# Layer 0's attention woven into its in-projection, modulation weights in half-sized parts, one copy moved

## The reference

```python
mod = silu(c) @ ada_w[i] + ada_b[i]              # 1024 -> 6 x 1024: sh1, sc1, g1, sh2, sc2, g2
h = rms_norm(x, norm1_g[i]) * (1 + sc1) + sh1
q, k, v = split(h @ w_in)                        # 1024 x 3072
a = softmax(q1 k1' - slopes*dist) - lam * softmax(q2 k2' - slopes*dist)   # 8 heads, two maps each
x = x + g1 * (rms_norm(a @ v, subln_g) * 0.8) @ w_out
h = rms_norm(x, norm2_g[i]) * (1 + sc2) + sh2
x = x + g2 * hierarchical_moe(h)                 # router, top 2 of 32 experts, 3 matrices of 2 MB each
```

## Time and profile before

| | |
|---|---|
| three runs | 1846.0, 1846.84, 1852.7 us (median 1846.84) |
| the profiled execution | 1846.84 us, its span 1845.0 us, mean clock of PE 0.972 |
| busy over the span | PE 91%, DVE 27%, ACT 24%, POOL 9% |
| moved by DMA | 585.12 MB, mean 317 GB/s |
| the chain that ended last | PE 60%, DMA 25%, DVE 6%, ACT 3%, issue 3%, SP's queue 3% |

### The profile page before, as it was taken

The page is one execution under the profiler, slowest core; times in us unless marked ns, Lnnn a source line. Parts: engine busy times, 40 slices in busy tenths (PEclk is TensorE's granted clock), DMA queues, the critical chain, the costliest instruction groups (busy, mean ns, idle before and its releaser), DMA issues.

```text
span 1845.0 us, 18530 instructions
## 1 busy us (share of the span) xinstructions
PE 1684.1 (91%) x7537; PEld 859.2 (47%) x7537; DVE 490.1 (27%) x935; ACT 444.2 (24%) x939; POOL 158.4 (9%) x236
## 2 busy tenths in 40 slices
PE   6896999888889879999999999999998999989988
PEld 4643543333333334845464344444443356565564
DVE  1357221000000103244241002221220123553362
ACT  2015211111111102015231013333331034343351
POOL 0212010000000010123000010000001000100000
PEclk9999999999999999999989999999998999999999
DMA  9989779999999999987369989999999963413310
GB/s 359 347 337 397 296 277 409 422 419 420 422 421 421 421 413 396 383 338 258 115 244 410 347 323 397 395 405 420 420 419 410 368 231 107 145 50 117 137 46 23
DMA packets 122752, 585.12 MB, mean 317 GB/s; under 512 B 11936, under 2 KB 16872, under 8 KB 99008
## 3 DMA queue, kind: packets, MB, share of 16 engines
q1 hardware_dynamic: 101008, 489.59, 66.3%
q0 software_dynamic: 21536, 88.72, 13.1%
q10 hardware_dynamic: 112, 5.51, 0.8%
HBM read 578.87 MB, written 21.32 MB: 325 GB/s over the span
## 4 chain that ended last, share of the span: by engine, by line
PE 60%; DMA 25%; DVE 6%; ACT 3%; issue 3%; SPq 3%; ACTq 0%; DVEq 0%; POOL 0%
PE psum L2204 57%; DMA ring<-in_expert_w_up 19%; DMA work<-in_ada_w 3%; SPq L1433 1%; PE psum L699 1%; DMA ring<-in_expert_w_gate 1%; SPq L1402 1%; DMA work<-in_ctx 1%; DMA ring<-in_ada_w 1%; DMA work<-in_w_mod 1%; PE psum L2508 1%; DVE small L1057 1%; PE psum L1198 1%; DVE work L1882 1%; DVE work L2099 0%
## 5 line engine op out<-in xcount | busy, mean ns | idle before, releaser
L2204 PE MATMUL psum<-ring,work 128*64 128x512 f32 (+5 forms) x4272 | 1095.4, 575 | 66.8 <-DMA ring<-in_expert_w_up 53.9
L2204 PEld LDWEIGHTS psum<-ring,work 128*64 128x64 f32 (+2 forms) x4272 | 424.3, 152 | 664.5 <-issue 635.0
L2204 PE MATMUL psum<-work 128*128 128x192 f32 (+9 forms) x1048 | 218.2, 371 | 8.1 <-DVE work L2032 2.6
L2204 PEld LDWEIGHTS psum<-work 128*128 128x128 f32 (+3 forms) x1048 | 144.9, 188 | 105.2 <-issue 81.6
L2099 DVE TENSOR_TENSOR work<-work,psum 128x256 f32<-128x256 f32 x64 | 27.0, 421 | 593.2 <-ACT work L1802 593.2
L1802 ACT ACTIVATE work<-psum 128x256 f32<-128x256 f32 x64 | 24.5, 383 | 607.7 <-PE psum L2204 607.7
L2204 PE MATMUL psum<-work,ring 128*128 128x256 f32 x704 | 158.8, 384 | 3.2 <-DMA ring<-in_diff_w_in 1.1
L2204 PEld LDWEIGHTS psum<-work,ring 128*128 128x128 f32 x704 | 133.4, 192 | 29.1 <-issue 8.1
L1669 ACT ACTIVATE work<-psum 128x256 f32<-128x256 f32 (+5 forms) x184 | 79.7, 443 | 224.7 <-PE psum L2508 76.0
L1561 POOL DMA_INDIRECT expert_rows<-work,targets x56 | 55.1, 984 | 806.6 <-DVE work L2125 806.6
L2125 DVE TENSOR_TENSOR work<-psum,rows 128x512 f32<-128x512 f32 x64 | 44.3, 692 | 255.8 <-PE psum L2204 255.7
(11 more groups left out here) (295 smaller groups left out, 956.6 us busy)
## 6 DMA issues: line engine op xcount, KB each, us to landing
ring<-in_expert_w_gate SPq DMA_DIRECT2D x60, 2048.0 KB, 16.5
ring<-in_expert_w_up SPq DMA_DIRECT2D x60, 2048.0 KB, 17.4
ring<-in_expert_w_down SPq DMA_DIRECT2D x57, 2048.0 KB, 14.4
work<-in_ada_w POOLq DMA_DIRECT2D x40, 1024.0 KB, 8.0
ring<-in_w_in SPq DMA_DIRECT2D x12, 2048.0 KB, 10.1
work<-in_w_mod POOLq DMA_DIRECT2D x16, 1024.0 KB, 6.8
ring<-in_sb_w_in SPq DMA_DIRECT2D x6, 2048.0 KB, 24.7
ring<-in_w_out SPq DMA_DIRECT2D x6, 2048.0 KB, 8.0
```

Of the source, the lines that this page charges most:

```text
L2204: return T.matmul(out_, lhsT, rhs, start=start, stop=stop, skip_group_check=True)
```

## The change

1. Layer 0's in-projection is split. `head` does blocks 0 to 4 (two of v, two of q, one of k); the other seven are cut into 14 halves and done inside the loop of the attention (`HALVES`: one in each of turns 0 to 7, three in turn 8, one in each of 9 to 11). w_in's slices are loaded in the order of use (`SLICES`). Until turn 12 the scores use one pair of banks, and a unit is turned two turns and multiplied three turns after its scores.
2. `ada_in` is seen as six buffers of 1024 columns for the summed groups (`ada_half`). Loads are 512 KB parts, sums go in 16 half steps per group (`ada_step` counts them), PE's item for a group is two items of two products. A part's load waits for half steps, except for the last part of each half sum (part numbers 7, 15, 23, 31), whose buffer is free only when PE has used the half sum (`half_free`).
3. On DVE only group 1's sum stands ahead of the first unit. Group 2's half steps go two to a turn in turns 0 to 7, `ada_take(1)` in turn 3, `ada_take(2)` in turn 10, `ada_take(3)` behind the attention.
4. PE's items of group 3 go to turns 11, 12, 13, 15, 17, 19 and behind the loop (22, 23); items 24 to 27 behind each of the four blocks of the projection.
5. SP: slices 5 and 6 of w_in at 12 half steps, w_out at 26, experts at 32 (before: 5, 13 and 24 by `ada_used`).
6. The copy to `expert_rows` waits for the first tile of the residual (`x_half`), and a buffer for squares (`o_sq`) is gone: its room holds a fourth buffer for scores, combined maps and turned maps.
7. In layer 1 the items of the two summed groups are halves too, behind blocks 4, 6, 8 and 11.

```diff
+    SLICES = (4, 0, 2, 5, 1, 3)
+    BLOCKS = (("v", 0, 0), ("v", 0, 1), ("q", 1, 0), ("q", 1, 1), ("k", 2, 0), ("k", 2, 1), ("v", 3, 0), ("v", 3, 1),
+              ("q", 4, 2), ("k", 5, 2), ("q", 4, 3), ("k", 5, 3))
+    LAST_USE = (1, 3, 5, 7, 10, 11)
+    WOVEN = 12
+    HALVES = [range(k, k + 1) if k < 8 else range(8, 11) if k == 8 else range(k + 2, k + 3) for k in range(WOVEN)]
+    READY = (5, 6, 10, 12)
...
             if l == 0:
-                sp.wait_ge(sem("ada_used"), KT * 3)
+                sp.wait_ge(sem("ada_step"), 4 * KT)
...
+        def half_free(part):
+
+            g = group_of(part // 2)
+            if g not in SUMMED:
+                pool.wait_ge(sem("ada_used"), used_by(g - 1) + part // 2 % KT + 1)
+            elif part % KT == KT - 1:
+                pool.wait_ge(sem("ada_used"), used_by(g - 1) + part // KT % 2 + 1)
+            else:
+                pool.wait_ge(sem("ada_step"), steps_by(part + 1))
...
+        def ada_sum(g, ts=range(2 * KT)):
+
+            for t in ts:
+                part = 2 * KT * (g - 1) + t
+                now, before, factor = ada_half[:, part % 6, :], ada_half[:, (part - 1) % 6, :], cond[:, 0, t % KT:t % KT + 1]
+                dve.wait_ge(sem(f"ada_in{part % 6}"), in_count(part))
+                if t % KT:
+                    dve.wait_ge(sem("ada_step"), steps_by(part - 1))
+                    ins = V.scalar_tensor_tensor(now, now, factor, before, ALU.mult, ALU.add)
+                else:
+                    ins = V.tensor_scalar(now, now, factor, None, ALU.mult)
+                ins.then_inc(sem("ada_step"), 1)
...
                 for k in range(16 + 2):
-                    if k == 11:
-                        ada_take(3)
+                    if 1 <= k <= WOVEN:
+                        diff_combine(k - 1)
                     if k < 16:
                         diff_scores(k)
-                    if k >= 2:
+                    if k >= WOVEN + 2:
                         diff_combine(k - 2)
+                    if k == 3:
+                        ada_take(1)
+                    if k < 8:
+                        ada_sum(2, [2 * k, 2 * k + 1])
+                    if k == 10:
+                        ada_take(2)
...
+        DIFF_ITEMS = [[] for k in range(16 + 4)]
+        DIFF_ITEMS[2], DIFF_ITEMS[6], DIFF_ITEMS[9] = [1], [KT], [KT + 1]
+        for at_, k in enumerate((11, 12, 13, 15, 17, 19)):
+            DIFF_ITEMS[k] = [2 * KT + at_]
+        PROJ_ITEMS = [24], [25], [26], [27]
...
             for k in range(16 + 4):
+                if k < WOVEN:
+                    for hb in HALVES[k]:
+                        woven_half(5 + hb // 2, hb % 2)
...
-                finite = a["expert_w_down"][0, 0:3].rearrange("e f d -> (e f) d")[0:TAIL * LIST, :]
-                act.dma_start(expert_rows, finite).then_inc(sem("rows_set"), 16)
             else:
                 stick_act(act, link, copy)
+            if l == 0:
+                act.wait_ge(sem("x_half"), 1)
+                finite = a["expert_w_down"][0, 0:3].rearrange("e f d -> (e f) d")[0:TAIL * LIST, :]
+                act.dma_start(expert_rows, finite).then_inc(sem("x_rows"), 16)
```

237 lines of the change are left out of this document (152 added, 85 removed).

## The result

The changed kernel took **1881.4 us** (median of 4, 1879.6 to 1887.4) against 1847.6 for the one before: ratio 1.0186, 95% interval 1.017 to 1.0202. The forecast was 1859, the range ended at 1869; the direction was right, the time outside. The profiled execution has a span of 1879.1, 34.1 more than before. I follow these 34 us through the trace.

What follows compares the result with a forecast made beforehand. The prediction took layer 0's experts to be bound by their weight stream, full DMA, so expert 0's start sets the time. Terms: -8.9 + 4.2 + 14.9 + 2 = +12.2 on 1846.84, so 1859 us; range 1838 to 1869.

Steps and rivals of the forecast that it cites:

- I cost them at nothing: Layer 1's in-projection: halving the items of two sums costs nothing, or 1 us if a half sum comes after its block.
- Gain of 10.9 in the attention: Layer 0's woven loop: first sum ends near 80, attention's last product at 170 instead of 180.67; bounds 161 and 176.
- Gain left 8.9: From attention to projection: items 21 to 23 cost 1 us and item 23's load 1, so the projection starts at 177.
- +14.9 at item 30: Ahead of the router's turning of x: PE waits for item 30's late load, 14.9 us; bounds +3.6 and +20.
- P+49: Forecast landing of item 30, P being the projection's start; P+45 with the copy harmless, P+54 by bytes.
- +4.2 for items 24 to 27: Inside layer 0's projection: four items behind its blocks, where PE is full, 0.95 each and their seams, add 4.2 us.
- Clock +2: After PE idles some 14 us at item 30, the lower clock costs 2 us behind it; bounds 0 and 5.
- 1:1 from expert 0 on: Layer 0's experts: their end moves one for one with the start of expert 0's products, 243.87 before.
- rival 1: Item 30's load is quick, under about 8 us: 1847 us, no slower; chance 0.2.
- Rival 2: The weave runs at its issue limit, POOL's waits hidden, and item 30's load is quick: 1837 us; chance 0.14.
- Rival 3: The weave gives nothing: 12 us landings in each POOL wait, low clock, attention ends at 180: 1870 us; chance 0.08.
- three POOL waits: Woven loop, POOL's in-order queue: part 21 about 1 us late, part 22 behind line 1's store about 6.5, part 29 3.5.

Runs made afterwards that it cites:

- e1: Changed kernel with layer 1's four half-sum items behind blocks 1, 4, 8, 11 instead of 4, 6, 8, 11: 1872.9 us.
- e10: Changed kernel with the woven attention's half-sum items and the additions to lines 1 and 2 moved to the turns where their sums are ready: 1874.2 us.
- e3: Changed kernel with the experts' first weights released again when item 23 has been used, not at 32 half sums: 1884.2 us.
- e13: e12 with the experts' first weights released again when item 23 has been used, not at 32 half sums: 1863.5 us.
- e12: e11 with item 31 behind the ranks' products in layer 0 and the second stream's norm behind the router's exponentials in layer 1: 1845.2 us.
- e18: e17 with expert 2's gate and up weights behind item 31 and the early down weights in SP's queue: 1850 us.
- e15: e14 with item 31 back behind the router's logits: 1858.6 us.
- e9: Changed kernel with the edits of e1, e2 and e8, items 22 to 24 and the third line's addition later, items 30 and 31 behind the logits: 1855.8 us.
- e2: Changed kernel with the copy to the row buffer back in its old place behind oT: 1873.3 us.
- e4: Changed kernel with items 29 and 30 moved on PE from ahead of the turning of x to behind the router's logits: 1871.6 us.
- e5: Changed kernel with the copy to the row buffer issued behind the router's exponentials instead of behind the first residual: 1874.9 us.
- e8: Changed kernel with the store of line 1 behind parts 22 and 23 in POOL's queue instead of in front: 1876.3 us.
- e11: e9 with e5's place for the copy and e10's turns, in the place of the edits of e2 and e8: 1845.4 us.
- e14: e12 with the copy issued right behind the scaling of x for the router: 1849.9 us.
- e17: e11 with only layer 1's second norm moved, to behind the router's exponentials: 1844.2 us.

## Why the prediction was wrong

- **"I cost them at nothing"** (layer 1's halves, 1 us if late): failed. In the in-projection +7.8, and e1 gave back 9.5 in the trace and 8.5 in the median. "Nothing" failed even without a wait: the 2.2 that stay are two more half items of 1.03. I looked at whether the half sum comes after its block, and not at who waits while it stands finished in its buffer: POOL, with all later parts behind it. In layer 0 I had reasoned so; in layer 1 I didn't follow the queue.
- **Gain of 10.9 in the attention**: the mechanism was right, the size wrong: 5.7. The first sum ended at 83.55 and not 80, and not by the part I followed: part 10 landed at 75.3 (15.8 us, where I took 8.4), and the last six half steps ran behind it without a wait, part 13 among them. The waits of turns 2 and 3 went on to PE and left its half blocks at the low clock. Part 29's wait was 6.35 and not 3.5, but it was covered by turn 8, as forecast (135.31 against 139.28). Unit 8 came at 139.90 against 133.3, and the lag stayed to unit 15 (166.13 against 159). e10 took all three waits away and gained 10.0 at the last product, 164.92. Read so, the loop without them is good for 15.8, between my bounds. (By its own numbers the forecast of 170 is a gain of 10.7, not 10.9; the 0.2 carries no weight.)
- **Gain left 8.9**: 0.6 was left. Of the difference 5.2 is the step before, 3.1 here: items 21 to 23 wait 2.9 in all with loads of 6.7 to 10.7 us. How much of this the early expert weights are, for which I had 1 to 2 as a bound, isn't shown: e3's 2.8 is within what traces of one program differ by. e13 shows that they are worth more than they cost.
- **+14.9 at item 30**: right in place and cause, 16.9 with item 29's. Item 30 landed at P+51.9, between my P+49 and the later end, P+54; the turning was at P+53.8 and not P+50. But the copy is a third of the wait: with item 30's load issued late, behind the last block, and gate and up beside it, 11.5 are there without the copy. The Trainium skill (DMA: Bandwidth & Descriptors, "Queues, rings and completion order") says that a DMA engine goes round its queues a packet at a time. The landings of 5.0 us alone, 12.6 beside gate and up and 19.6 beside the copy agree with it.
- **+4.2 for items 24 to 27**: 4.1. **Clock +2**: 3.7, of which 1.9 are items 29 and 30 (1.89 each where 0.95 was reckoned) and 1.8 the way from turning to expert 0.
- **1:1 from expert 0 on**: right, 489.9 before, 490.3 after, and 489.5 to 490.4 in the others, except in e12 (495.1), e13 (498.0) and e18 (500.6), where PE waits for a late weight, and e15 (491.5).
- Rivals: rival 1 decides at a landing under 8 us; it was 19. Rival 2's place, turn 3, had its wait. Rival 3's 1870 was the nearest, but not for its reason: landings in the three POOL waits took 4 to 9 us, not 12, and the attention ended at 175, not 180.

By terms: -0.6 for -8.9, +22.9 for +19.1, +1.8 for +2, +9.9 for 0. Layer 1 makes 10 of the 22 us of error, and the attention with its way to the projection 8. Open: the 2.2 us at layer 1's router. ACT waits there for the second stream's input (4.03, before 2.87) with the exponentials behind it. The wait is 2.17 in e1, 1.94 in e10 and 3.88 in e9, and from turning to expert 0 it takes 28.8 to 31.7 us in e1, e2, e4, e5 and e8 to e11, whose edits don't touch layer 1's router; so the 2.2 may be no more than what executions differ by.

## What to carry to other kernels

When a change alters which step frees a buffer, follow the queue that refills it, in every place where the change does so: what matters isn't when the consumer needs the sum, but when its buffer comes free and what is queued behind. A finished sum goes out in the first slot behind its completion. And price a stall by where it can be moved: here 10 of 17 us only changed place, and what removed the rest was a sooner load. Splitting a small product into two isn't free even where nothing waits: each half cost as much as the whole.

## What the runs showed that I had not expected

- Time of a 1 MB load by its company: 5.0 us alone, 12.6 beside two queued loads of 2 MB, 19.6 beside the 5.5 MB copy, 31.6 beside both and behind another item's load in its own queue (e14).
- That copy costs the stream nothing behind the router's exponentials (e5), leaves 3 us of wait if the early down weights are issued 5 us behind it (e12; in e11 and e17, 3 us behind, none), and 13 to 18 us of wait if an item's load is still on its way when it starts (e14, e15).
- The same early release is worth 18.4 us in the repaired kernel; in the changed one its 2.8 aren't clear of noise. What a load costs depends on which other wait already covers it.
- With its losses repaired the woven attention brings expert 0 forward by 2.6 us, and the time of the kernel isn't told apart from one without it.
